# A one-layer decoder trunk on one core: the second norm's gain and bias applied by columns, two more buffers lent to early expert weights, a nine-place ring kept for five pairs of experts, and the residual added in the eleventh pair

## The reference, cut to what matters

```
h = hybrid_mixer(x, w_in[l], b_forget[l], w_mix_out[l], rel_bias)
x = layer_norm(DEEPNORM_ALPHA * x + h, ln1_g[l], ln1_b[l])
h = memory_cross_attention(x, mem, w_cq[l], w_ck[l], w_cv[l], w_co[l])
x = layer_norm(DEEPNORM_ALPHA * x + h, ln2_g[l], ln2_b[l])
h = moe_ffn(x, w_router[l], b_router[l], w_gate_up[l], b_gate_up[l], w_down[l], b_down[l])
x = layer_norm(DEEPNORM_ALPHA * x + h, ln3_g[l], ln3_b[l])
```

## Time and profile before

| what | us |
|---|---|
| median of three runs (1204.27 to 1204.81) | 1204.78 |
| span of the profiled execution | 1202.1 |
| the profiled execution's own time, by its span and the 2.7 us that the median lies above it | 1204.8 |
| PE busy | 1146.8 (95%) |
| DVE busy | 219.4 (18%) |
| ACT busy | 133.3 (11%) |
| POOL busy | 49.7 (4%) |
| share of the 16 transfer engines taken by SP's queue | 88.3% |
| mean granted TensorE clock | 0.995 |

### The profile page before, as it was taken

How to read it: one execution, slowest core, us unless ns; L and a number is a source line. 1 busy time by engine, 2 the same in 40 slices (tenths; PEclk the granted TensorE clock), 3 DMA queues, 4 the chain that set the end, 5 groups by cost and what they waited for, 6 DMA issues and landing times.

```text
span 1202.1 us, 12962 instructions
## 1 busy us (share of the span) xinstructions
PE 1146.8 (95%) x5354; PEld 522.3 (43%) x5354; DVE 219.4 (18%) x559; ACT 133.3 (11%) x281; POOL 49.7 (4%) x56
## 2 busy tenths in 40 slices
PE   9999999999999999999999999898989899999986
PEld 7686747754434343433434343333333333333322
DVE  1232122224211111121111111111111111111113
ACT  2133111222100000010000000000000000000001
POOL 0232002010000000000000000000000000000001
PEclk9999999999999999999999999999999999999998
DMA  9953334398999999999999999999999999999995
GB/s 350 323 204 141 133 112 157 122 373 326 429 429 427 427 414 429 428 429 430 427 429 427 427 428 429 429 430 427 428 428 430 429 429 427 429 430 429 427 429 215
DMA packets 55698, 446.63 MB, mean 372 GB/s; under 512 B 10304, under 2 KB 11472, under 8 KB 30192
## 3 DMA queue, kind: packets, MB, share of 16 engines
q1 hardware_dynamic: 53200, 440.49, 88.3%
q10 hardware_dynamic: 2464, 5.66, 1.3%
HBM read 445.06 MB, written 1.07 MB: 371 GB/s over the span
## 4 chain that ended last, share of the span: by engine, by line
PE 62%; DMA 35%; DVE 2%; issue 1%; SPq 0%; ACT 0%
DMA ring<-in_w_gate_up 32%; PE bank L1693 21%; PE bank L1333 9%; PE bank L1742 9%; PE bank L1320 8%; DMA ring<-in_w_down 3%; PE bank L1577 3%; PE bank L1638 2%; PE bank L1653 1%; PE bank L1367 1%; PE bank L1718 1%; PE bank L1792 1%; PE bank L1731 1%; PE bank L1519 1%; PE bank L1497 1%
## 5 line engine op out<-in xcount | busy, mean ns | idle before, releaser
L1693 PE MATMUL bank<-ring,PT 128*64 128x512 f32 x1792 | 396.5, 594 | 29.9 <-DMA ring<-in_w_gate_up 29.9
L1693 PEld LDWEIGHTS bank<-ring,PT 128*64 128x64 f32 x1792 | 125.9, 137 | 295.3 <-issue 235.4
L1182 DVE TENSOR_SCALAR reg_k<-bank 128x512 f32<-128x512 f32 x32 | 22.1, 691 | 449.9 <-PE bank L1693 444.1
L1320 PE MATMUL bank<-reg_bc,ring 128*128 128x256 f32 x448 | 99.6, 381 | 0.0
L805 ACT ACTIVATE reg_v<-reg_k 128x512 f32<-128x512 f32 x30 | 18.9, 630 | 689.3 <-DVE reg_k L1182 689.3
L1742 PE MATMUL bank<-reg_q,NCt 128*64 128x512 f32 x400 | 92.0, 602 | 0.0
L1320 PEld LDWEIGHTS bank<-reg_bc,ring 128*128 128x128 f32 x448 | 84.4, 190 | 14.1 <-issue 3.2
L1742 PE MATMUL bank<-reg_bc,NCt 128*64 128x512 f32 x400 | 90.1, 592 | 0.0
L1577 PEld LDWEIGHTS bank<-L,reg_a 128*128 128x128 f32 x512 | 62.9, 196 | 24.8 <-issue 23.5
L1577 PE MATMUL bank<-L,reg_a 128*128 128x128 f32 x512 | 69.3, 288 | 1.0 <-DVE L L1096 0.7
L1213 DVE COPY reg_v<-bank 128x512 f32<-128x512 f32 x28 | 19.4, 692 | 269.0 <-PE bank L1742 269.0
(11 more groups left out here) (232 smaller groups left out, 709.0 us busy)
## 6 DMA issues: line engine op xcount, KB each, us to landing
ring<-in_w_gate_up SPq DMA_DIRECT2D x114, 2048.0 KB, 23.3
reg_bc<-in_w_down SPq DMA_DIRECT2D x26, 2048.0 KB, 20.7
reg_q<-in_w_down SPq DMA_DIRECT2D x25, 2048.0 KB, 19.2
ring<-in_w_down SPq DMA_DIRECT2D x8, 2048.0 KB, 18.9
ring<-in_w_in SPq DMA_DIRECT2D x5, 2048.0 KB, 17.1
reg_kv<-in_w_gate_up SPq DMA_DIRECT2D x5, 2048.0 KB, 18.0
ring<-in_w_down SPq DMA_DIRECT2D x9, 1024.0 KB, 7.3
reg_q<-in_w_gate_up SPq DMA_DIRECT2D x4, 2048.0 KB, 14.2
```

The source lines that it names most:

```text
L1182: nc.vector.tensor_scalar(gbuf, banks[0][:, :], LIMIT, None, ALU.min).then_inc(g_ready, 1)
L1320: last = mm(B(name)[:, a * T:(a + 1) * T], w[:, k, c:c + P], src[:, k, :], start=(k == 0), stop=(k == KD - 1))
L1693: last = mm(ps[half * CAP:(half + 1) * CAP, :], xgT[:, k, i * CAP:(i + 1) * CAP], w[:, j, col:col + HALF], start=(opens and k == 0), stop= ...
```

## The change

1. Gain and bias of the second norm are no longer applied to the tokens. `x2hat` (in `reg_v`, in place of `x1`) holds the row less its mean over its deviation, by four ACT instructions (tile 1's now after the table load for Exp). POOL's four and DVE's four instructions for gain and bias go, and so do the two transfers of 512 KiB. Gain and bias come as columns (`lncol[:, 4]` and `[:, 5]`, two small transfers), and are applied when the gathered tokens leave their banks: `evac_xgT` has four ACT instructions of 128 columns with a scale and a bias each, where it had one copy of 512 columns. For the first pair ACT does this for slices 0 to 3 and DVE for 4 to 7.
2. `reg_a` and `x_nat` are free after the first norm. `lent` has three half chunks: slices k = 0 and k = 1 of expert 0 in `reg_a` and `reg_k`, and k = 6 of expert 1 in `x_nat`. The first expert's products go in the order k = 2 to 7, 1, 0.
3. `OPEN` is 5: the nine places serve five pairs. `OPENING` begins in another order; the halves at the start and the counters of landings follow it.
4. `BASE_PAIR` is 10. There the residual is made from `x2hat`: POOL builds two tables `diag` in `x_nat` (the scaled identity times the gain of each column, and times the bias); for each half of the columns PE spreads the gains over a bank (L1625), adds the bias part to both tiles of `acc`, DVE multiplies the bank into `x2hat` (`scaled_residual`), and PE adds that to `acc` by the identity. The rest of the base follows.
5. The third norm's gain and bias are loaded behind the last expert's weights. `ysb`, `sig`, `repT` move from `reg_v` to `reg_a`, the output `y3` from `reg_a` to `reg_v`.

```diff
-BASE_PAIR = 6
+BASE_PAIR = 10
...
-OPEN = 2 * NSLOT // CH
-OPENING = ([(i, c) for i in range(2) for c in range(GUC)] + [(i, c) for i in range(2) for c in range(GUC, CH)]
+OPEN = 5
+OPENING = ([(1, 3), (0, 1), (0, 2), (0, 3), (1, 0), (1, 1), (1, 2), (0, 4), (0, 5), (1, 4), (1, 5)]
            + [(e, c) for e in range(2, OPEN * 2) for c in range(CH)])
...
-        y3 = mem_nat
+        y3 = reg_v
+        diag = x_nat[:, :, :].rearrange("p s (k f) -> p s k f", k=KD)
...
+        x2hat = reg_v
+        scaled_x2 = (gbuf, sig)
...
+        lent = {(0, 0): reg_a[:, :], (0, 1): reg_k[:, :], (1, 6): x_nat[:, :, :].rearrange("p a d -> p (a d)")}
...
-                    load_half(NSLOT, 0, ahead_in)
+                    load_half(NSLOT, 0, ahead_in[0])
+                    wait_evacuated(sp, ("wo1", 1))
+                    load_lent(1, 6)
+                    sp.wait_ge(ln_out, TT)
+                    load_lent(0, 0)
                     continue
                 if n == NSLOT - 1:
-                    sp.dma_start(lent, chunk_source(0, 0)[:, 0:1, :]).then_inc(lent_in, 16)
+                    load_lent(0, 1)
                 load_chunk(*OPENING[n], n)
...
             for c in range(CH):
-                wait_opening(OPEN * 2 * CH - NSLOT + c)
+                wait_opening((OPENED[c] - 1) * NSLOT + c)
                 load_chunk(OPEN * 2, c, c)
...
+            pool.wait_ge(gu_done, 2 * BASE_PAIR - 1)
+            for i in range(2):
+                last = nc.gpsimd.tensor_tensor(
+                    diag[:, i, :, :], K[:, C_AID:C_AID + P].rearrange("p (k f) -> p k f", k=1).to_broadcast([P, KD, P]),
+                    lncol[:, 2 + i, :].rearrange("p (k f) -> p k f", f=1).to_broadcast([P, KD, P]), ALU.mult)
+            last.then_inc(diag_ready, 1)
...
-                nc.scalar.activation(xgT[:, 4 * half:4 * half + 4, :],
-                                     (xy_ps, tr_ps)[half][:, :].rearrange("p (k c) -> p k c", k=4),
-                                     ACT.Copy).then_inc((xgTa_sb, xgTb_sb)[half], 1)
...
+                for j in range(4):
+                    k = 4 * half + j
+                    last = nc.scalar.activation(xgT[:, k, :], (xy_ps, tr_ps)[half][:, j * P:(j + 1) * P], ACT.Identity,
+                                                scale=lncol[:, 4, k:k + 1], bias=lncol[:, 5, k:k + 1])
+                last.then_inc((xgTa_sb, xgTb_sb)[half], 1)
...
+            def scaled_residual():
+
+                dve.wait_ge(h_ready, 2 * BASE_PAIR + 1)
+                for half in range(2):
+                    cols = slice(half * HALF, (half + 1) * HALF)
+                    dve.wait_ge(gain_done, half + 1)
+                    if half > 0:
+                        dve.wait_ge(scaled_used, half)
+                    for tt in range(TT):
+                        last = nc.vector.tensor_tensor(scaled_x2[tt], xy_ps[:, :], x2hat[:, tt, cols], ALU.mult)
+                    last.then_inc(scaled_ready, 1)
...
+                pe.wait_ge(diag_ready, 1)
+                pe.wait_ge(y_sb, p * 2)
+                for half in range(2):
+                    rows = slice(4 * half, 4 * half + 4)
+                    if half > 0:
+                        pe.wait_ge(scaled_ready, half)
+                    mm(xy_ps[:, :], one, diag[:, 0, rows, :].rearrange("p k f -> p (k f)"),
+                       start=True, stop=True).then_inc(gain_done, 1)
+                    for tt in range(TT):
+                        mm(acc[tt][half][:, :], one, diag[:, 1, rows, :].rearrange("p k f -> p (k f)"),
+                           start=False, stop=False, skip_group_check=True)
+                    pe.wait_ge(scaled_ready, half + 1)
+                    for tt in range(TT):
+                        last = mm(acc[tt][half][:, :], ident, scaled_x2[tt], start=False, stop=False, skip_group_check=True)
+                    last.then_inc(scaled_used, 1)
                 pe.wait_ge(rep_ready, 1)
...
-                for tt in range(TT):
-                    for half in range(2):
-                        mm(acc[tt][half][:, :], K[:, C_AID:C_AID + P], x2[:, tt, half * HALF:(half + 1) * HALF],
-                           start=False, stop=False, skip_group_check=True)
                 pe.wait_ge(cand_ready, 1)
```

More of the change, by code:

```diff
@@ L347, in hybrid_layer @@
         slot_in = [sem(f"slot_in{n}") for n in range(NSLOT)]
-        lent_in, ahead_in, ahead2_in = sem("lent_in"), sem("ahead_in"), sem("ahead2_in")
-        ahead3_in, ahead4_in, opened = sem("ahead3_in"), sem("ahead4_in"), sem("opened")
+        lent_in = {at: sem(f"lent_in{at[0]}_{at[1]}") for at in lent}
+        ahead_in = [sem(f"ahead_in{k}") for k in range(5)]
+        xg1_act, xg1_dve = sem("xg1_act"), sem("xg1_dve")
+        opened = sem("opened")
         piece_in = [sem(f"piece_in{j}") for j in range(len(PIECES))]
@@ L769, in normalise @@
                 act.wait_ge(nmr_ready, tt + 1)
-                nc.scalar.activation(x2[:, tt, cols], x1[:, tt, cols], ACT.Identity, scale=rstd[:, 1, tt, 1:2],
-                                     bias=nmr[:, tt:tt + 1]).then_inc(xn_ready, 1)
+                wait_filled(act, ("rT", tt, half))
+                nc.scalar.activation(x2hat[:, tt, cols], x1[:, tt, cols], ACT.Identity, scale=rstd[:, 1, tt, 1:2],
+                                     bias=nmr[:, tt:tt + 1]).then_inc(x2hat_ready, 1)
             def four(name):
@@ L776, in _ @@
             std(1, 0)
+            copy(("rT", 0, 0), rT[:, 0:4, :], four(("rT", 0, 0)))
             for half in range(2):
                 normalise(0, half)
-            copy(("rT", 0, 0), rT[:, 0:4, :], four(("rT", 0, 0)))
             copy(("rT", 1, 0), rT[:, 0:4, :], four(("rT", 1, 0)))
@@ L1206, in pair @@
                     if with_base and i == 0:
+                        scaled_residual()
                         further_blocks()
@@ L1602, in base @@
             def base(p):
+                pe.wait_ge(diag_ready, 1)
+                pe.wait_ge(y_sb, p * 2)
+                for half in range(2):
+                    rows = slice(4 * half, 4 * half + 4)
[10 more added lines that the diff above has]
+                    last.then_inc(scaled_used, 1)
                 pe.wait_ge(rep_ready, 1)
-                pe.wait_ge(y_sb, p * 2)
                 for j in range(2):
@@ L1695, in gate_up @@
                                       skip_group_check=True)
+                    if (i, k, opens) == (1, 0, True):
+                        last.then_inc(opened, 1)
                     if j == GUJ - 1 and k < KD - 1:
@@ L1703, in first_gate_up @@
             def first_gate_up():
-                pe.wait_ge(xgTa_sb, 1)
-                for k in (1, 2, 3, 0, 4, 5, 6, 7):
-                    if k == 4:
-                        pe.wait_ge(xgTb_sb, 1)
+                order = (2, 3, 4, 5, 6, 7, 1, 0)
+                for k in order:
+                    for n, evacuations in enumerate(((2, 3, 1, 0), (4, 5, 6, 7))):
+                        if k in evacuations:
+                            pe.wait_ge((xg1_act, xg1_dve)[n], evacuations.index(k) + 1)
                     c, j = k // GUJ, k % GUJ
-                    if k == 0:
-                        pe.wait_ge(lent_in, 16)
-                        w = lent
+                    if (0, k) in lent:
+                        pe.wait_ge(lent_in[0, k], 16)
+                        w = lent[0, k]
                     else:
-                        w = chunk(0, 0, c, "open")
+                        w = chunk(0, 0, c, "open")[:, j, :]
                     for ps, c0 in zip((gate_ps, up_ps), (0, F)):
```

163 lines of the change are left out of this document (71 added, 92 removed).

## The result

The changed kernel takes **1209.22 us** (median of four runs, 1206.13 to 1211.62) against 1204.53 us of the kernel before on the same chip: a ratio of **1.0038**, 95% interval 1.0025 to 1.005. Slower, by 4.7 us; 1208.6 us and "slower" had been forecast. One thing was not: over these four runs each the kernel before stays within 0.9 us, the changed one spreads over 5.5 us. Its profiled execution is its fastest, 1206.13 us with a span of 1203.8.

A forecast was written before the change was run, and what follows sets the result against it. Loads set the end, counted from the last time the queue runs dry for lack of a free place. 1204.8 + 0.5 (second stall) + 3.3 (third) = 1208.6 us; range 1204.2 to 1211.8, the likeliest case's own 1205.8 to 1210.8.

The forecast's parts named there:

- last dry spell: Last time the load queue lacks a free place; the end follows from that load's issue, a start and 4.89 us per chunk.
- Start of the experts: Before the first product: DVE's bias instruction goes, gaining 0.24 us of PE; ACT's new normalising is hidden, else up to 1.6 us late.
- First stall: Near 331 to 336 us, waiting for (1,4): most of the extra early chunk's 4.89 us is given back.
- Evacuations: Four ACT instructions for one in each pair: 0.7 us lost (bounds 0.3 and 0.9), a pair of 54.6 us.
- Second stall: At the change to six places, (10,3) waits for (9,4) until 551.2; queue 0.5 us later (1.1 earlier to 1.3 later).
- Third stall: At pair 10's base, grown by 7.4 us, the queue runs dry and loses 3.3 us (1.1 to 4.7).
- the prediction's own rule: At the base: landing to next load, plus 2.55 us to start, may take 29.35 us; anything longer is lost.
- DVE's chain: In pair 10's base, after the table transposes, nothing covers DVE's work on the tables: PE idles 2.1 us.
- the row of 5.0 us: A queue found empty lands 1 MiB 5.0 us after issue, 2.45 of it transfer, so 2.55 to start.
- The clock as a rival of 0.05: In pair 10's base the clock may fall to half, or PE not catch up: 1213.5 us; chance 0.05.
- The end: The end comes by a landing, not PE's work; the sum starts from the profiled execution, put at 1204.8 us.

The follow-up runs named there:

- e3: The changed kernel with the residual's ten products in pair 8 and the rest of the base in pair 10; 1204.43 us, ratio 0.9999.
- e6: The changed kernel with the residual's ten products moved between the table transposes and the product that waits for cand; 1205.61 us, ratio 1.0004.
- e8: The kernel before with four ACT evacuations of 128 columns, scale 1 and bias 0, instead of one copy of 512; 1205.15 us, ratio 1.0002.
- e4: The kernel before with its base in pair 10 instead of pair 6, all else the same; 1205.1 us, ratio 1.0003.
- e11: e9 without the half chunk lent in x_nat, so one chunk fewer loaded before the first product; 1206.03 us, ratio 1.0011.
- e9: The changed kernel with the nine places kept for twelve pairs (OPEN = 12); 1205.54 us, ratio 1.0008.
- e7: The kernel before with six products of 512 columns more in its base, written to a bank that nothing reads; 1204.99 us, ratio 1.000.
- e1: The changed kernel with the nine places kept for six pairs instead of five; 1208.02 us, ratio 1.0029.
- e2: The changed kernel with one 512-column evacuation again from the second pair on, without gain and bias; 1207.95 us, ratio 1.0027.
- e12: The changed kernel with residual in pair 8, nine places for six pairs, and x_nat lent again for half a chunk of expert 3; 1202.2 us, ratio 0.9981.

## Why the prediction was right, point by point

- **What bounds, and counting from the last dry spell.** Held. The three dips stand where they were put, and taking the third away (e3, e6) takes back 4 to 4.8 us. Only e8, where the last dry spell came 1.5 us later and the median did not follow, speaks against it.
- **Start of the experts.** ACT's normalising was hidden. The first product stood at 284.10 instead of 284.72, but in profiles of other variants it stands at up to 286.50 (e4), so 0.24 us can't be read from it.
- **First stall: the extra chunk is given back.** Held: 92 GB/s from 330 to 335, and 0.5 to 1.0 us left of 4.89 (e11 against e9), though by halving the stall and not by ending it.
- **Evacuations: 54.6 us a pair.** Measured 54.56, and 1.51 us for four instructions again, so 0.35 from start to start. By the figures of the Trainium skill ("ScalarE: Activation LUTs", "What ACT_TABLE_LOAD costs") with two pointer operands it is 186 + 107 + 186 - 93 ns, an estimate of 0.39 us and not the 0.37 of the prediction, and a pair 0.15 us longer than by the row; the row decides.
- **Second stall: (10,3) at 551.2, 0.5 us behind the kernel before.** Issued at 550.8. (The count for the kernel before gives 550.7, where the prediction writes 550.8.) e3 and e6, which have only the first two stalls, stand at 0.0 and 0.65 us against the kernel before, where 0.5 was said; the landing in front of pair 10's base is 0.5 us ahead of the kernel before (853.36 against 853.87) in the first profile and level with it (853.88) in the second.
- **Third stall: mis-sized.** The base was to grow by 7.4 us, bounds 5.2 and 8.8. From landing to load it was 28.4 us in the first profile instead of 30.1, and 30.0 in the second (853.88 to 883.87). What parts them is a fall of the clock, and the base before has one too:

```profile
634.66 2.08 PE L1653 MATMUL bank<-L 64*128 64x512 f32 x4
636.67 4.27 PE L1742 MATMUL bank<-reg_q,NCt 128*64 128x512 f32 x16
```

  The same rows take 1.13 and 3.65 us in the earlier trace rows, so that fall cost 1.6 us, of which the prediction saw the 0.72 from 634 to 636. I took it as part of the base and added the growth to it; it comes and goes. Like for like the growth was right: 30.0 - 22.7 = 7.3 us. The loss was not. It was 2.7 and 4.4 us by the 30th slice of the two profiles (389 and 366 GB/s), where the prediction's own rule makes 1.6 and 3.2 us of 28.4 and 30.0. The rule counts the landing of the last of the 16 engines; its own landings come 2.0 and 3.4 us late behind the base (6.9 and 8.3 us after the one before instead of 4.89). The first engine is 2.1 us ahead of it, and the engines ahead run dry sooner. In the medians the stall is worth 4.8 us (against e3). By e6 the order that uncovers DVE's chain, one term of 2.1 us in the sum, was worth most of it. By the Trainium skill ("DMA: Bandwidth & Descriptors", "Latency and other measured facts") the stall would have been an estimate of 1.3 us; the measured 2.7 and more go with the row of 5.0 us.
- **The clock as a rival of 0.05.** It was not a rival but a part of the forecast's own term: 22.69 us hold one fall. The 5.5 us between the runs had no place in the text. With no margin left at that wait a fall goes into the end, as the two profiles show for one fall; that the slower runs have two is not shown.
- **The end.** It came by landings and the chain behind them, not by PE's work: PE waits for weights again from 1037 us on. The last products come 2.8 us later than before in the first profile (1191.49 against 1188.72 us by the chains), while its time is 1.3 us above the 1204.8 that I set for the profile of before. Runs of the kernel before have a time 1.8 us above their span (1204.19 and 1202.4), so its profiled execution is nearer to 1203.9 than to the median's 1204.8; the sum started 0.9 us too high. And the end itself is shorter than before, which the sum did not have: from the last DVE instruction to the end of the span it is 3.06 us in each of the two profiles of the changed kernel, and 3.8 to 4.1 in the four of the kernel before, e4, e7 and e8. No run says why.
- **The number.** That 1208.6 us came within 0.6 us of the median is partly luck. In medians the start is 1204.5 us and not 1204.8, all but the third stall makes 0.0 us (e3, the shorter end included) where 0.5 was said, and the third 4.8 where 3.3 was said; the errors partly cancel.

## What to carry to other kernels

Where a queue of loads sets the time, price an edit by the margin that it leaves at each wait for a place, not by its own length: 8.6 us of work in a pair with some 13 us to spare cost nothing (e3); in the pair of the base the same work cost 0.5 us in an order that covers DVE's chain (e6), and 4.7 us in one that leaves PE 1.9 us to wait for it. Look for what a product covers before moving it, and leave margin for a fall of the clock at the end of short products and waits. Weights loaded ahead pay only if the places do not run out at the same wait; a buffer for that very wait does.

## What the runs showed of the hardware that had not been expected

- **Instruction fetches** on the transfer engines, as told under e9 to e11: 1.5 to 1.8 us for the engine that is hit, 1.2 to 1.5 us for the landing that PE waits for where that engine is among the last; 26 packets before, 30 after, 41 with twelve pairs unrolled.
- **POOL beside DVE.** POOL builds `diag` in pair 9, while DVE works on the swiglu, and DVE's product of two tiles takes 2.39 us, where it took 0.69 a pair earlier:

```profile
770.42 0.69 DVE L1201 TENSOR_TENSOR reg_k<-reg_k,reg_a 128x512 f32<-128x512 f32 x1
...
800.34 2.39 DVE L1201 TENSOR_TENSOR reg_k<-reg_k,reg_a 128x512 f32<-128x512 f32 x1
```

```profile
798.43 3.75 POOL L630 TENSOR_TENSOR x_nat<-K,lncol 128x1024 f32<-128x1024 f32 x2 [519.56 <-PE bank L1715]
```

  PE then waits, and the granted clock is 0.59 from 804 to 808 us. Pair 9 has margin, so it cost no transfer. The Trainium skill ("SBUF — State Buffer", "SBUF: two separate sides") says that a DVE instruction with two SBUF inputs and a GpSimd one that reads SBUF take turns at a shared pair of ports, each holding it for its whole length; the trace agrees: POOL's second instruction ends at 798.43 + 3.75 = 802.18, and with 0.69 us from there DVE would end at 802.87; it ends at 802.73.
- **The same fall of the clock, or none, on the same instructions**: in pair 10 none in the first profile of the changed kernel, one in the second (876.9 to 880.3), from the same wait for `ctl` of 0.73 us. Nine profiles show a wait of 1.86 or 2.10 us for `cand`; in four of them (e1, e2, e3, e12) the clock falls right behind that wait, in five it does not. What parts the runs is open.
